# A hybrid decoder block on one core: the forgetting gates ride on the first value projection

## The reference, cut to what matters

```
xr, gr, q, k, v, fl, mg = jnp.split(z, split_idx, axis=-1)      # 1280 1280 1024 1024 1024 8 2048
...
log_f = jax.nn.log_sigmoid(fl.astype(jnp.float32) + b_fgate[l].astype(jnp.float32))
F = jnp.cumsum(log_f, axis=1)                                    # per head, along the tokens
s = (q * Dh**-0.5) @ k.T + F[query] - F[key], masked, softmax, times v
```

## Time and profile before

| what | value |
|---|---|
| median of three runs | 985.53 us (985.08 to 988.39) |
| the profiled execution | 988.54 us |
| its span, from first to last instruction | 986.7 us |
| PE busy | 969.3 us, 98% |
| DVE busy | 637.6 us, 65% |
| ACT busy | 420.9 us, 43% |
| mean granted clock of PE | 0.991 |

### The profile page before, as it was taken

The page is one execution under the profiler, slowest core; times in us unless marked ns, Lnnn a source line. Parts: engine busy times, 40 slices in busy tenths (PEclk is TensorE's granted clock), DMA queues, the critical chain, the costliest instruction groups (busy, mean ns, idle before and its releaser), DMA issues.

```text
span 986.7 us, 12710 instructions
## 1 busy us (share of the span) xinstructions
PE 969.3 (98%) x4727; PEld 815.4 (83%) x4727; DVE 637.6 (65%) x858; ACT 420.9 (43%) x552; POOL 2.2 (0%) x12
## 2 busy tenths in 40 slices
PE   7999999999999999999999999999999999999997
PEld 7977888788888888989888889888888888888875
DVE  3779999622568787863758555777764443754665
ACT  6478778422425354352723383332223222422331
POOL 0000000000000000000000000000000000000000
PEclk7999999999999999999999999999999999999999
DMA  9733322233764445332126515566533232223201
GB/s 329 243 97 96 96 74 69 76 96 100 235 214 143 149 154 193 128 107 86 57 72 227 190 53 171 172 205 200 189 111 102 90 123 85 86 98 136 106 18 68
DMA packets 105774, 129.36 MB, mean 131 GB/s; under 512 B 4636, under 2 KB 81156, under 8 KB 105612
## 3 DMA queue, kind: packets, MB, share of 16 engines
q1 hardware_dynamic: 105192, 126.75, 39.2%
q10 hardware_dynamic: 548, 2.14, 0.7%
HBM read 126.77 MB, written 2.11 MB: 131 GB/s over the span
## 4 chain that ended last, share of the span: by engine, by line
PE 86%; DVE 8%; issue 3%; ACT 1%; DMA 1%; SPq 1%; DVEq 0%; ACTq 0%
PE ps L1646 28%; PE ps L1647 27%; PE ps L1648 27%; DVE xc L1162 2%; DVE wsplit L990 1%; PE ps L1880 1%; PE ps L1705 1%; DMA ada_first<-in_w_ada 1%; PE ps L1722 1%; PE ps L1688 1%; DVE wsplit_x L1549 0%; DVE wraw_x L1545 0%; DVE xrs L1169 0%; PE ps L1698 0%; ACT htmp L654 0%
## 5 line engine op out<-in xcount | busy, mean ns | idle before, releaser
L1646 PE MATMUL ps<-h,wsplit 128*128 128x512 f32 (+1 forms) x816 | 313.1, 384 | 3.1 <-ACT gl L716 1.5
L1648 PE MATMUL ps<-h,wsplit 128*128 128x512 f32 (+1 forms) x816 | 310.9, 381 | 0.0
L1647 PE MATMUL ps<-h,wsplit 128*128 128x512 f32 (+1 forms) x816 | 310.8, 381 | 0.0
L990 DVE TENSOR_TENSOR wsplit<-wraw,wsplit 128x2048 fp32r<-128x2048 f32 (+2 forms) x79 | 166.9, 2114 | 100.5 <-ACT wsplit L604 62.9
L1646 PEld LDWEIGHTS ps<-h,wsplit 128*128 128x128 f32 x816 | 153.5, 188 | 33.6 <-issue 4.9
L1648 PEld LDWEIGHTS ps<-h,wsplit 128*128 128x128 f32 x816 | 153.4, 188 | 29.7
L1647 PEld LDWEIGHTS ps<-h,wsplit 128*128 128x128 f32 x816 | 153.5, 188 | 28.5
L604 ACT ACTIVATE wsplit<-wraw 128x2048 fp32r<-128x2048 f32 (+2 forms) x69 | 120.9, 1752 | 102.0 <-PE ps L1648 101.8
L1575 DVE SCALAR_TENSOR_TENSOR cv<-ps,vec,cv 128x511 f32<-128x511 f32 (+1 forms) x48 | 35.9, 748 | 55.7 <-ACT cv L947 52.6
L1041 DVE SCALAR_TENSOR_TENSOR ada_acc<-ada_raw,small,ada_acc 128x512 f32<-128x512 f32 x84 | 63.1, 751 | 2.7
L1646 PE MATMUL ps<-wsplit,act_s 128*128 128x512 f32 x160 | 62.3, 390 | 0.7 <-DVE act_s L1562 0.7
(11 more groups left out here) (261 smaller groups left out, 1422.9 us busy)
## 6 DMA issues: line engine op xcount, KB each, us to landing
wraw<-in_w_ffn_up SPq DMA_DIRECT2D x24, 1024.0 KB, 5.1
wraw<-in_w_in SPq DMA_DIRECT2D x23, 1024.0 KB, 5.3
ada_raw<-in_w_ada SPq DMA_DIRECT2D x16, 1024.0 KB, 6.7
wraw<-in_w_ffn_down SPq DMA_DIRECT2D x10, 1024.0 KB, 4.9
ada_first<-in_w_ada SPq DMA_DIRECT2D x8, 1024.0 KB, 10.4
ada_raw<-in_w_ada_final SPq DMA_DIRECT2D x8, 1024.0 KB, 5.1
wraw<-in_w_in SPq DMA_DIRECT2D x12, 512.0 KB, 3.9
wraw<-in_w_proj_rnn SPq DMA_DIRECT2D x8, 640.0 KB, 4.3
```

What stands on the lines that cost most here:

```text
L990: ve.tensor_tensor(wsplit[:, s, LO, 0:n], wraw[:, s, 0:n], wsplit[:, s, HI, 0:n].bitcast(F), ALU.subtract).then_inc(w_lo, 1)
L1646: te.matmul(dst, lhs(LO), rhs(HI), start=start, stop=False)
L1647: te.matmul(dst, lhs(HI), rhs(LO), start=False, stop=False)
L1648: return te.matmul(dst, lhs(HI), rhs(HI), start=False, stop=stop)
```

## The change

1. The 24 matmuls of the forgetting gates in the merge stage are gone. The 8 columns (`fw`) are appended to the first value chunk, in tiles of their own (`vw`, 264 columns), split by ACT and DVE beside it.
2. Step 0 of attention goes values, queries, keys. The first value projection (`v_first`) writes four PSUM banks of 264 columns each, so PE waits until all gate products of the merge stage have left the banks (`mixa_done`, KD).
3. The log sigmoid runs on 128 partitions × 32 values in place of 8 × 512. Its result is transposed four times to 8 × 512 for the scan (new), and `nF` back four times as before, both between projections of step 0.
4. The store and re-read of `nF` moves on SP from behind the third chunk of step 0 to behind the loads of the modulation weights in `load_step(4)`.
5. DVE's order in step 0 is changed with it: the pieces of `ada2`, `gate1_store` and the last `qk_lo`.

```diff
@@ SP
-            load(C_ATT, 0, cols_of(w_in_v, COL_Q, 256), KD, 256)
-            load(C_ATT + 1, 0, cols_of(w_in_v, COL_K, 256), KD, 256)
-            load(C_ATT + 2, 0, cols_of(w_in_v, COL_V, 256), KD, 256)
-            sp.wait_ge(fl_step, 6)
-            sp.dma_start(nF_dram, nF[:, :]).then_inc(nF_stored, 16)
-            sp.wait_ge(nF_stored, 16)
-            load_nF(0)
+            load(C_ATT, 0, cols_of(w_in_v, COL_V, 256), KD, 256)
+            load(C_ATT + 1, 0, cols_of(w_in_v, COL_Q, 256), KD, 256)
+            load(C_ATT + 2, 0, cols_of(w_in_v, COL_K, 256), KD, 256)
...
                 load_ada2(i4 // 2 + 3)
+                if i4 == 4:
+                    sp.wait_ge(fl_step, 7)
+                    sp.dma_start(nF_dram, nF[:, :]).then_inc(nF_stored, 16)
+                    sp.wait_ge(nF_stored, 16)
+                    load_nF(0)
@@ ACT
-            ae.wait_ge(small_loaded, 32)
-            ae.activation(fws[:, HI].rearrange("p k h -> p (k h)"),
-                          fw[:, :, :].rearrange("p k h -> p (k h)"), ACT.Copy).then_inc(fw_hi, 1)
@@ PE
             te.wait_ge(gelu_done, NR)
-            te.wait_ge(fw_lo, 1)
-            for k in range(KD):
-                ins = mm3(ps[0:H, 3, :], lambda part: fws[:, part, k], features(h, k), k == 0, k == KD - 1)
-            ins.then_inc(fl_mm, 1)
             proj_rnn(C_MIX + 2, 2, 0, lambda k: te.wait_ge(y_part, 2 * k + 2))
...
+            def v_first():
+                te.wait_ge(w_lo, whole(C_ATT))
+                te.wait_ge(fw_lo, 1)
+                for b in range(NB):
+                    for k in range(KD):
+                        ins = mm3(ps[:, b, 0:256 + H], lambda part: h[:, part, k, P * b:P * b + P],
+                                  lambda part: vw[part][:, k], k == 0, k == KD - 1)
+                    if b == 1:
+                        ins.then_inc(tile0, 1)
+                ins.then_inc(w_used, 1)
...
             te.wait_ge(sigr_done, KD)
+            te.wait_ge(mixa_done, KD)
+            v_first()
+            te.wait_ge(att_lo, 1)
+            te.wait_ge(fl_step, 1)
             qk_proj(0, 0, 0)
-            te.wait_ge(mixa_done, KD)
             qk_proj(0, 0, 1)
...
+            te.wait_ge(fl_step, 6)
+            for b in range(NB):
+                ins = te.transpose(ps[0:H, 3, P * b:P * b + P], fl1[:, b], ident[:, :])
+            ins.then_inc(fl_mm, 1)
```

More of the change, by code:

```diff
@@ L772, in _ @@
             hi(C_MIX + 15, 0, NR * P)
[L774 to L778, removed]
+            ae.wait_ge(w_loaded[C_ATT % 2], landed(C_ATT))
+            ae.wait_ge(w_used, C_ATT + 1)
+            ae.activation(vw[HI][:, :, 0:256], wraw[:, C_ATT % 2].rearrange("p (k n) -> p k n", k=KD), ACT.Copy)\
+              .then_inc(w_hi, 1)
+            ae.wait_ge(small_loaded, 32)
+            ae.activation(vw[HI][:, :, 256:256 + H], fw[:, :, :], ACT.Copy).then_inc(fw_hi, 1)
             def qk_hi(i, t, which):
-                c0 = C_ATT + which
+                c0 = C_ATT + which + (1 if isinstance(i, int) and i == 0 else 0)
                 if t == 0:
@@ L796, in v_hi, with v_first_hi @@
                               ps[:, half, :], ACT.Copy).then_inc(att_hi, 1)
+            def v_first_hi(half):
+                if half == 0:
+                    ae.wait_ge(tile0, first(C_ATT))
+                else:
+                    ae.wait_ge(w_used, whole(C_ATT))
+                ae.activation(vh[:, HI, 2 * half:2 * half + 2], ps[:, 2 * half:2 * half + 2, 0:256], ACT.Copy)\
+                  .then_inc(att_hi, 1)
             def gate_a(i, t):
@@ L1330, in v_lo, with v_first_lo @@
                   .then_inc(att_lo, 1)
+            def v_first_lo(half):
+                two = slice(2 * half, 2 * half + 2)
+                ve.wait_ge(att_hi, 1 + half)
+                ve.tensor_tensor(vh[:, LO, two], ps[:, two, 0:256], vh[:, HI, two].bitcast(F), ALU.subtract)\
+                  .then_inc(att_lo, 1)
+                if half == 0:
+                    ve.wait_ge(small_loaded, 32)
+                ve.tensor_tensor(fl1[:, two], ps[:, two, 256:256 + H],
+                                 bfg[:, :].rearrange("p (a h) -> p a h", a=1).broadcast_to([P, 2, H]), ALU.add)\
+                  .then_inc(fl_step, 1)
             def scores_add(i, t):
@@ L1822, in _ @@
             proj_rnn(C_MIX + 15, 1)
-            te.wait_ge(fl_step, 6)
-            for b in range(NB):
-                ins = te.transpose(ps[:, 3, H * b:H * b + H], nF[:, P * b:P * b + P], ident[0:H, 0:H])
-            ins.then_inc(nFq_mm, 1)
             def qk_proj(i, which, t):
-                c0 = C_ATT + which
+                c0 = C_ATT + which + (1 if isinstance(i, int) and i == 0 else 0)
                 if t == 0:
@@ L1919, in _ @@
             te.wait_ge(sigr_done, KD)
+            te.wait_ge(mixa_done, KD)
+            v_first()
+            te.wait_ge(att_lo, 1)
+            te.wait_ge(fl_step, 1)
             qk_proj(0, 0, 0)
[L1921 removed]
             qk_proj(0, 0, 1)
[L1923 to L1925 removed]
+            te.wait_ge(att_lo, 2)
+            te.wait_ge(fl_step, 6)
+            for b in range(NB):
+                ins = te.transpose(ps[0:H, 3, P * b:P * b + P], fl1[:, b], ident[:, :])
+            ins.then_inc(fl_mm, 1)
+            te.wait_ge(att_lo, 3)
+            qk_proj(0, 1, 0)
+            te.wait_ge(fl_step, 7)
+            for b in range(NB):
+                ins = te.transpose(ps[:, 2, H * b:H * b + H], nF[:, P * b:P * b + P], ident[0:H, 0:H])
+            ins.then_inc(nFq_mm, 1)
+            te.wait_ge(att_lo, 4)
             qk_proj(0, 1, 1)
             ada_total(4, 7, ada2_split)
[L1928 removed]
+            te.wait_ge(att_lo, 5)
             with te.Fori(1, H // 2 - 1) as i:
```

95 lines of the change are left out of this document (49 added, 46 removed).

## The result

The changed kernel took 990.4 us (median of 14 runs, 989.59 to 992.85), the kernel before on the same chip 987.71 us (14 runs, 983.28 to 989.77): ratio 1.0031, 95% interval 1.0018 to 1.0045. So it is slower by some 0.3%, just where a difference can be told from none, and the forecast of 987.1 us (984.6 to 989.2) missed. A second series of it gave 990.87 us and 1.0027.

A forecast was written before the change was run, and what follows sets the result against it. PE, busy 98%, was taken to bound the kernel, with DVE binding in the merge stage. Terms -0.29 - 0.24 + 1.20 + 0.32 + 0.60 = +1.59 us on 985.53 gave 987.1 us, range 984.6 to 989.2.

The forecast's parts named there:

- The 24 gate matmuls: Merge stage: of 5.53 us taken off PE, 5.2 become waits for DVE; gain 0.29 us.
- The split at 57 us: Gates' weights at 57 us: ACT loses an operation DVE's chain waits for, so all moves by 0.24 us; gain 0.24.
- The border wait: Border to attention: PE's first value matmul waits for the last gate product; cost 1.20 us, bounds 0.9 and 1.5.
- 264 columns: Value projection in step 0: 96 matmuls of 264 columns in place of 256 cost 0.32 us.
- The transposes: Step 0 of attention: four new transposes of 128 columns cost 0.60 us, bounds 0.45 and 0.87.
- Step 0, DVE and SP: Step 0 into step 1: DVE's later work and SP's store and re-read, 4.9 us apart, are covered; no cost.
- Rival C: Step 1: `nF` or the query chunk lands 3 to 4 us late, costing 1 to 2 us; chance 0.08.
- The sum: Whole kernel: -0.29 - 0.24 + 1.20 + 0.32 + 0.60 = +1.59 us; span from 986.7 to 988.3.
- Rival B: Merge stage near 186 us: PE's stalls lower the clock, losing 1.7 to 5.1 us (988.8 to 992.2); chance 0.15.
- The level: Whole kernel: the change put on the median of the runs before, 985.53 + 1.6 = 987.1 us.

The follow-up runs named there:

- after: The changed kernel itself, against the kernel before: 990.4 us median, ratio 1.0031; profiled execution 990.34 us.
- after_p2: The changed kernel unaltered, a further single profiled execution: 988.57 us.
- e7_after_keep: The changed kernel with unread 512-column matmuls (7, 7, 4 and 1) in PE's merge-stage stalls: 988.26 us, ratio 1.0012 to the kernel before.
- e7_again: The kernel of e7_after_keep once more, word for word: 990.91 us median, ratio 1.0017 to the kernel before.
- e2_banks: The changed kernel with the first value projection in PSUM banks 4 to 7, its gate-product wait moved behind it: 988.75 us, ratio 1.0001 to the kernel before.
- after_again: The changed kernel unaltered, timed again as a second series: 990.87 us median, ratio 1.0027 to the kernel before.
- e4_pool: The kernel of e2_banks with GpSimd making the LO parts of three chunks in place of DVE: 993.6 us, ratio 1.0044 to the kernel before.

## Why the prediction missed, step by step

- **The 24 gate matmuls, -0.29: right.** From the restart to the last merge matmul 127.90 before, 127.64, 127.59, 127.62 and 127.61 in the four profiles of the changed order there without the half clock (after, after_p2, e7_after_keep, e7_again): -0.26 to -0.31. The waits, their enders and the 0.14 + 0.10 of a restart are in the rows.
- **The split at 57 us, -0.24: nearly right.** DVE's `lru_w` waits 0.82 us for ACT as before; from PE's last start ahead of the wait near 66 us to the restart near 139 it is 74.02 us before (139.48 - 65.46) and 73.84 after (139.80 - 65.96): -0.18. It is 73.97 to 74.02 in all three profiles with the split at the old place and 73.80 to 73.89 in the eleven others.
- **The border wait, +1.20: right.** 268.72 - 267.44 - 0.227 = 1.05, and the second matmul 0.08 late: 1.13. e2_banks takes away 1.07.
- **264 columns, +0.32: mis-sized.** From 268.92 to 280.41 are 95 matmuls, 0.1209 us each, for 0.1200 at 256: 0.09 us for 96. The line between the rows for 256 and 512 columns does not hold for 8 columns.
- **The transposes, +0.60: a little high.** 291.97 - 291.07 - 2 x 0.227 = 0.45 us. The Trainium skill (TensorE: Matmul & The Clock Gate, Part 4: PE-mode transpose) gives about 275 ns for one in context; four in a row cost 0.45 us here, so the row read as distance was the better guide.
- **Step 0, DVE and SP: right in effect, SP wrong in size.** No wait of PE stands between 268.8 us and the scores. The re-read of `nF` followed its store by 1.5 us and not by 4.9. It waits for the store to land, 4.4 us before and 1.2 after, by SP's waits. Before, a chunk of 1 MB had been issued 0.42 us ahead of the store; after, the transfer engines were idle when it went out. So the prediction took for the price of the transfer alone, and as one "when nothing competed", what was the price behind a chunk; that the chunk made the difference is the likely reading and was not tested. `scores_add` began 2.54 us after the scores (306.22 - 303.68), forecast 2.7. Rival C did not happen.
- **The sum, +1.59: measured +1.27** (-0.18 - 0.29 + 1.74, the last from 719.32 to 721.06). The two small terms were 0.4 us too high between them; the other three were right within 0.1. By the starts 1.70 of the 1.74 us lie before the first scores (34.54 us from the last merge matmul before, 36.24 after).
- **Rival B, chance 0.15: this step failed.** It was described well ("it may do so in some executions only") and priced at 1.7 us and more; it came in 2 of 4 profiles of the changed kernel, at 1.1 to 1.2 us, as part of the 3.4 us lay over PE's waits. The forecast put it at nothing in its sum and gave it 0.15 as a case that is there or not. With what the profiles show, a share of one half and 1.2 us, it is a term of +0.6 us in the mean; even by its own chance and price it was one of 0.3.
- **The level: this step failed.** "Put on the median of the runs, 985.53 + 1.6": those three runs lay low in the lottery of the start. Over all series the kernel before has a mean of 988.0 us (105 runs, 983.3 to 991.0). With it, 988.0 + 1.3 + 0.6 = 989.9; all 26 runs of the changed kernel have a mean of 990.5 ± 0.6. The range of 984.6 to 989.2 was laid around a centre 2.5 us too low. By the medians of the first series this step is the larger part of the miss: of the 3.3 us (990.4 for 987.1) 2.2 are the kernel before itself (987.71 for 985.53), and 1.1 are the change (2.69 for 1.6). A range 2.2 us higher would have held the result.

What stays open: the changed kernel stands 2.3 and 3.35 us above the kernel before in two series, and structure with the half clock explains 1.9. The rest is within the uncertainty of the means, but both lie on the same side. The runs' clocks say what it is made of: in the series of after_again the changed kernel stood at half clock for 17.8 us in the mean and the kernel before for 15.3, which by the line above is worth 1.2 us, and with the +1.1 beside that line it gives the 2.3. They do not say where in the run: that the half clock comes behind the stalls oftener than in 2 of 4, or that the start was slower in these runs, by chance or not, stays open.

## What to carry to other kernels

A matmul before a wait can be free: before one is taken off a busy PE, find on the engine that feeds it the end that PE waits for next, and expect that end and not PE's time to set the gain. Idle time put between short bursts on PE can cost more than its own length, through the clock, in some executions and not in others (here 0.8 to 1.4 us); give it a share in the sum. Where a few runs scatter by more than the effect, compare distances between two fixed instructions of two traces, which repeat within about 0.1 us here, lay the runs against their granted clock, and take the level from all the runs there are.

## What the hardware did that was not expected

- Where GpSimd's elementwise operation had started first, DVE's operation ended only behind it, in all three places of e4_pool: a cast of 2.45 us for 0.43, two products of 4.03 for 1.29, a scan of 3.31 for 1.22. The Trainium skill (GPSIMD Engine Reference, 1. Specifications) says that GpSimd's SBUF interfaces are shared with VectorE. This trace agrees, and its rows look like waiting for the whole of GpSimd's operation and not like sharing: behind its end DVE needed 0.3, 1.2 and 1.1 us, about what the work takes alone.
- The granted clock fell to half some 0.4 us behind the last of three stalls of 1.6, 1.5 and 0.8 us (after_again, near 186.0), and stayed there for 3.4 us, in which PE was busy, while it held in other executions with the same stalls.
- The start phase, with the clock at 0.89 or 0.97 over its 60 us, moves this kernel's time by up to 6.6 us (restart at 134.37 to 141.02).
